# Splitting the four feature products of each joint-stretch step into two and two, half a step apart

## Time and profile before

| | |
|---|---|
| runs | 1484.68, 1479.36, 1479.19 us; median 1479.36 |
| profiled execution | 1482.81 us, of which 1481.0 us are the span of the trace |
| busy in the span | PE 1302.6 (88%), DVE 677.5 (46%), POOL 449.0 (30%), ACT 294.3 (20%) |
| chain that ended last, by engine | PE 66%, DVE 12%, issue 7%, ACT 4%, DMA 4% |
| features (L1619), 1152 instructions | 542.1 us busy |
| mean granted TensorE clock | 0.948 of full speed |

### The profile page before, as it was taken

The page is one execution under the profiler, slowest core; times in us unless marked ns, Lnnn a source line. Parts: engine busy times, 40 slices in busy tenths (PEclk is TensorE's granted clock), DMA queues, the critical chain, the costliest instruction groups (busy, mean ns, idle before and its releaser), DMA issues.

```text
span 1481.0 us, 20692 instructions
## 1 busy us (share of the span) xinstructions
PE 1302.6 (88%) x7189; PEld 670.1 (45%) x7189; DVE 677.5 (46%) x1095; ACT 294.3 (20%) x648; POOL 449.0 (30%) x358
## 2 busy tenths in 40 slices
PE   3999999996997997796977897299999969999999
PEld 3444344453553553453434443155555533554443
DVE  4445304657667667573635546634433104343101
ACT  3112013334324334232111110011212011001000
POOL 0122202534334434343645562354551000000000
PEclk9899999998998999998999998599999989989999
DMA  8020406655775664575898789378685374252121
GB/s 264 22 101 31 151 0 229 194 184 164 223 228 173 221 201 165 179 250 165 253 296 293 250 290 349 83 237 302 225 302 201 115 231 129 96 189 87 57 86 58
DMA packets 167181, 269.25 MB, mean 182 GB/s; under 512 B 29618, under 2 KB 66297, under 8 KB 165916
## 3 DMA queue, kind: packets, MB, share of 16 engines
q1 hardware_dynamic: 107636, 149.64, 31.8%
q10 hardware_dynamic: 59440, 118.28, 23.9%
HBM read 221.63 MB, written 46.40 MB: 181 GB/s over the span
## 4 chain that ended last, share of the span: by engine, by line
PE 66%; DVE 12%; issue 7%; ACT 4%; DMA 4%; ACTq 3%; SPq 2%; POOL 1%; DVEq 0%; POOLq 0%
PE ps L1619 22%; PE ps L1566 11%; PE ps L1926 7%; PE ps L1903 5%; PE ps L1642 3%; PE ps L1669 2%; PE ps L1702 2%; DVE sc L1205 1%; ACTq L872 1%; DMA work<-in_cache_v 1%; DVE qkv L1374 1%; SPq L599 1%; PE ps L1731 1%; ACTq L875 1%; PE ps L1734 1%
## 5 line engine op out<-in xcount | busy, mean ns | idle before, releaser
L1619 PE MATMUL ps<-hT,wbuf 128*128 128x512 f32 x1152 | 542.1, 616 | 0.0
L1619 PEld LDWEIGHTS ps<-hT,wbuf 128*128 128x128 f32 x1152 | 218.5, 198 | 237.5 <-issue 234.8
L697 POOL TENSOR_TENSOR prod<-work,qB 128x512 f32<-128x512 f32 x128 | 172.7, 1363 | 198.9 <-DVE sc L1205 130.4
L697 POOL TENSOR_TENSOR prod<-kbuf,qB 128x512 f32<-128x512 f32 x128 | 163.8, 1298 | 115.0 <-DVE sc L1205 90.4
L1205 DVE TENSOR_REDUCE sc<-prod 128x8 f32<-128x512 f32 x256 | 167.3, 677 | 6.5 <-POOL prod L697 6.0
L1566 PE MATMUL ps<-wbuf,hT 128*128 128x512 f32 x384 | 167.3, 596 | 0.0
L1566 PEld LDWEIGHTS ps<-wbuf,hT 128*128 128x128 f32 x384 | 72.8, 191 | 91.3 <-issue 91.2
L1926 PE MATMUL ps<-hT,work 128*128 128x512 f32 x256 | 110.3, 592 | 0.0
L1903 PE MATMUL ps<-qkv,wbuf 128*128 128x512 f32 x192 | 91.6, 632 | 15.4 <-issue 11.0
L1926 PEld LDWEIGHTS ps<-hT,work 128*128 128x128 f32 x256 | 48.5, 190 | 60.7 <-issue 60.7
L1642 PE MATMUL ps<-work,pr 128*2 128x128 f32 x2048 | 69.9, 272 | 6.2 <-DMA work<-in_cache_v 6.2
(11 more groups left out here) (325 smaller groups left out, 1351.2 us busy)
## 6 DMA issues: line engine op xcount, KB each, us to landing
work<-in_cache_v ACTq DMA_DIRECT2D x256, 256.0 KB, 4.1
kbuf<-in_cache_k SPq DMA_DIRECT2D x128, 256.0 KB, 3.5
work<-in_cache_k SPq DMA_DIRECT2D x128, 256.0 KB, 3.9
wbuf<-in_w_main ACTq DMA_DIRECT2D x10, 2048.0 KB, 9.3
gsp<-work SPq DMA_DIRECT2D x24, 512.0 KB, 4.2
feat_dram<-qkv ACTq DMA_DIRECT2D x20, 512.0 KB, 4.3
qkv<-in_x_prompt SPq DMA_DIRECT2D x16, 512.0 KB, 4.8
feat_dram<-fst ACTq DMA_DIRECT2D x32, 256.0 KB, 3.5
```

The lines of the kernel that those rows point to most:

```text
L697: nc.gpsimd.tensor_tensor(prod[:, p % 4, :], kslot[u], qB[:, j % 2, :], ALU.mult).then_inc(s["page_mul"], 1)
L1619: ins = nc.tensor.matmul(ps[:, 4 + n % 2, :], wbuf[:, wb, kk, f * P:(f + 1) * P], hT[:, kk, half_ * W:(half_ + 1) * W], start=(kk == 0), s ...
```

## The change

In PE's `chunk(j)` a second yield stands between the second and the third product of every step, with a due time half a step later. In even steps kk runs from 0 to 3 and in odd steps from 4 to 7, so the condition holds once in each step. No other engine's program and no due time of another stream is touched.

```diff
                 for kk in range(k % 2 * KD // 2, (k % 2 + 1) * KD // 2):
+                    if kk % 4 == 2:
+                        yield slot(j, k + 0.5)
                     ins = nc.tensor.matmul(ps[:, 4 + n % 2, :], wbuf[:, wb, kk, f * P:(f + 1) * P], hT[:, kk, half_ * W:(half_ + 1) * W],
                                            start=(kk == 0), stop=(kk == KD - 1))
```

## The result

The changed kernel takes 1437.24 us (median of 4 runs, 1435.79 to 1442.67) against 1479.28 for the kernel before (4 runs, 1477.48 to 1484.68): a ratio of 0.9715, 95% interval [0.9685, 0.9744]. It is faster by 42 us, twice the 21 that were forecast, and beyond the lower end of the range (1441). The profiled execution took 1436.39 us with a span of 1434.6. The mean granted clock is 0.952 (0.948 before).

A forecast was written before the change was run, and what follows sets the result against it. PE was taken to carry the path, its idle time being what could be won. Terms 10.4 + 9.9 + 5.0 - 3.5 = 21.8 off 1482.81 gave 1461.0; the runs' median, 3.45 lower, gave 1458 us, range 1441 to 1480.

The forecast's parts named there:

- All cover holds: Rival, whole kernel: every covered wait goes, breaks cost nothing, 37 us plus 4 for less clock lowering: 1438 us; chance 0.11.
- the scan: 958 to 1204 us: eight waits of the second lifting step (5.6 us) go; taken as 5.0.
- the clock: Rival, first two stretches: finer groups lower the granted clock from 0.95 to 0.92, 20 us lost: 1478; chance 0.04.
- the round trip: 892 to 958 us, DMA round trip and DVE's inversion: no order of PE's work shortens them; no term.
- the groups' stretch: 675 to 892 us: covered waits sum to 16.6 us, of which 9.9 is taken; ends 4 and 16.6.
- the discount: Groups, 675 to 892 us: DMA as second bound, pages asked for sooner, so 60% of 16.6 us is taken, 9.9.
- key transposes, squares and scaled keys: Groups: waits of 6.7 + 6.9 us shrink to 7.7, a gain of 5.9; groups 2 and 5 get worse.
- the key-query products: Groups: their waits, 4.5 us, are covered by a half step of feature products after the decay.
- Attention's stretch: 233 to 675 us: covered waits sum to 15.6 us; bounded by 5 and 15.6 for loops, 10.4 taken.
- the seams: Attention, between heads, 20.3 us of waits: 1.7 gained at the first seam, 0 at the second, others keep their order.
- The breaks: Feature products: runs of eight rows broken once more in 78 of 144 steps, 0 to 15 us; 3.5 taken as cost.
- the 1.85: Groups' end: last key-query products move ahead, but a key load holds SP's store until 881.74, so only 1.85 us is won.

The follow-up runs named there:

- the three parts alone: The split only in attention's chunks, only in the groups' two, or only in the scan's, against 1480.35 us before: 1465.64, 1454.43 and 1473.99 us.
- the added traffic: The changed kernel, with SyncE loading another 128 KB into an unread tile in each of the groups' 32 steps: 1440.99 us (0.9745).
- quarters: The changed kernel with a due time for each of the four products, a quarter step apart: 1443.57 us (0.9767).
- the spread loads: The changed kernel with ScalarE's eight value-page loads at a chunk's start issued two by two over four steps: 1413.78 us (0.9539).
- the phase by stage: The changed kernel with the spread loads, and the product pairs half a step sooner in chunks 0 to 3 alone: 1405.21 us against 1414.0 without that.

## Why the prediction was wrong

**Direction and mechanism were right.** Most of the short waits went as listed, the long loop that was measured kept its length (8.17 and 8.16 us in group 6), and the three parts alone paid. The rival "All cover holds" (1438, chance 0.11) has the right number, but not by its terms: it counts 15.6 us in attention, 16.6 in the groups, 5.0 in the scan, 4 for the clock and nothing in the round trip, where the traces give 13, 25, 3 and 6. That the sums meet is luck.

**The step that failed is the groups' stretch, and in it the discount**: "Here DMA is the second bound ... Products that run sooner ask for pages sooner. I take 60%, 9.9". The stretch gave 25 us. The row of 1.01 was read as a bound. But PE's longest waits in that very stretch of the kernel before, 783 to 810 us, are for ScalarE and none is for a page:

```profile
PE ps L1764 <- ACT qkv L999: 3.7, 1, 3.7
PE ps L1734 <- ACT qkv L994: 1.1, 1, 1.1
```

And the same share in the changed kernel goes with a PE that does not stand still. Two short stretches of it, in the columns of the earlier trace rows:

```profile
706.00:720.00 14.00, 13.66 (x99) 7.60 (x99) 10.08 (x17) 2.58 (x3) 8.69 (x7) 1.00 1.00 310
720.00:735.00 15.00, 14.95 (x105) 7.46 (x106) 4.20 (x7) 3.35 (x6) 8.10 (x7) 1.00 1.05 396
```

PE is busy for 28.6 of 29 us at DMA shares of 1.00 and 1.05, and the added traffic cost 4 us and not 13.6. Here busy transfer engines cost time only where somebody waited for their data. In the earlier trace rows that was 5.2 us, and these went away where I had feared that they would grow. The reason given was the wrong way round: the page products stand behind the second pair, so they come later against the loads that ScalarE issues, as the prediction's own paragraph on queues says ("page products, later by the pieces that pass them"). The runs fit that, for the page waits also go when all products come later without a split (1.2 us and 0), and grow when the split comes sooner (9.3).

**The discount is not all of the miss.** Without it the sum is 28.5 and the forecast 1451 us. The span shrank by 24.6 us more than the 21.8 forecast; the discount makes 6.7 of these, and terms that the sum put at nothing make more: the value pages (5.2), less busy time in the groups (7.5) and the round trip (6). The first reading had let the pages slip: of PE's 98 idle us it names 39 and 49, and the 5.2 are in neither.

By terms, in the groups: key transposes, squares and scaled keys were forecast to give 5.9 and gave 6.0 (6.9 + 6.7 to 7.6); the key-query products 4.5 and gave 3.3; the next group's transpose 2.9 as forecast; the waits for L999 1.4 and gave nothing. That is 12.2 of 14.7 us, and the pages' 5.2 and the busy time's 7.5 make it 25. Of the 7.5, a clock of 0.98 for 0.95 on 183 us would make up to 5.5. But that is partly the luck of two traces: in chunks 4 and 5 the clock is 0.95 to 0.96 in five traces of the old order and 0.96 to 0.98 in six of the new, 0.96 the most frequent in both, and these chunks take 228.6 to 233.4 and 208.6 to 210.8 us. So the groups' gain is rather 21 than 25.

The clock stood in a rival alone, once in each direction. The Trainium skill, "TensorE: Matmul & The Clock Gate", section "A second HAM failure mode: psum-queue depth-cycling", tells of a kernel where short idle times between groups of matmuls made the clock swing between its two levels. No run here shows that for finer groups: the mean clock is 0.948 before, 0.952 with halves, 0.953 with quarters.

**Attention's stretch: the value was near, the reason for the size half right.** 10.4 was taken from 15.6, and PE's idle time fell by 11.4. As forecast, some came back in the loops, but little: 21.6 to 23.2 us of waits, where the discount was 5.2. The value products kept 4.1 us in three waits, not 1.43 in one; the seams gave 3.7, not 1.7. That these misses nearly cancel is luck. With 1.6 less busy time the stretch gained 13.

**The breaks** were to cost 3.5 on the path. The feature rows' own busy time grew by 10, inside the bounds of 0 to 15, but PE's busy time in the four stretches fell from 839.6 to 827.2: so whatever the breaks cost on the path is not to be seen beside what shrank otherwise; no run shows the 3.5.

**The round trip** had no term: "no order of PE's work shortens them" was wrong by 6 us, of which the way from the last key-query products explains 4.1: 1.9 on SyncE's side, the 1.85 that stood in the groups' sum, and 2.1 by the order of two loads. The rest depends on where the window was cut, at chunk 6's start.

**The scan** was to give 5.0. Its waits of 5.6 went and the idle time fell by 5.2 (8.3 to 3.1), but PE was busy some 2 us longer (237.7 to 240.0, with the end of the window 0.9 us late), and it gave 3 to 4: the breaks may show there.

Not settled are the cost of later features in attention (the runs were 23 and 38 us slower) and how the groups' gain divides between split and phase, for no run moves the page products alone. The waits for value pages themselves hold: they are 3.9 to 5.2 us in the groups in five traces of the old order.

## What to carry to other kernels

Where engines run fixed lists, count the dependent neighbours on the busiest engine that have no independent work between them, and spread the work that is there evenly over them: same work, other order, 3%. Where that work stands against the other engines is a second choice, to be made stage by stage (8.8 us here). Take a discount for "the next bound" only from a row in which somebody waits for it. And look at what a queue's owner cannot do while it issues transfers: eight loads in a row on an engine that also computes cost more than half of what the whole reordering gained.

## What the runs showed of the hardware

- ScalarE takes about 1 us to issue one of these page loads (seven in 6.98 us), each with a register load ahead of it, and computes nothing meanwhile. Spread over four steps the same loads cost 22 to 28 us less. The Trainium skill's section on issuing engines (named above) calls the time to initiate a DMA "usually small relative to the DMA itself". Here it is 1 us beside the 4.1 us that such a load takes to land.
- Where waits went, the granted clock rose and the same work took less busy time. In chunks 0 to 3 the clock is 0.95 with the change, 0.97 with the spread loads and 0.99 with the phase by stage, and PE is busy for 376.0, 371.4 and 367.1 us. The split alone does not show it: over the whole span single executions have 0.943 to 0.958 before and 0.949 to 0.954 with the change.
- A 512 KB load took 8.0 us when issued 1.2 us behind a 2 MB load, 6.6 at 0.4 behind, and 5.1 and 5.4 when ahead of it.
